# Products with stationary weights: one run of four loads per job instead of two runs of two

## What is computed

```
first_block:  h = x + (mixers(rms_norm(x) @ w_in, mem @ w_mem_kv) * gate) @ w_out
              u = relu(rms_norm(h) @ w_up)            # w_up   2048 x 8192
              h = h + (u * u) @ w_down                # w_down 8192 x 2048
second_block: m = hgrn2(rmsnorm(h) @ hgrn_w_in) @ hgrn_w_out
              x = h + rmsnorm(m)
              gate, value = conv3(rmsnorm(x) @ ffn_w_in)   # 2048 x 11264, centred, over tokens
              x = x + rmsnorm((silu(gate) * value) @ ffn_w_out)
```

## Time and profile before

| | |
|---|---|
| median of 3 runs | 2496.82 us (2496.26 to 2497.27) |
| the profiled execution | 2497.42 us |
| its span, first to last instruction | 2495.6 us |
| PE busy with matmuls | 2476.8 us, 99% of the span |
| PE loading weights | 2116.1 us, 85% |
| DVE busy | 1752.0 us, 70% |
| ACT busy | 1258.2 us, 50% |
| mean granted clock of PE | 0.997 |
| DMA | 466 MB, 187 GB/s |

### The profile page before, as it was taken

How to read it: one execution, slowest core, us unless ns; L and a number is a source line. 1 busy time by engine, 2 the same in 40 slices (tenths; PEclk the granted TensorE clock), 3 DMA queues, 4 the chain that set the end, 5 groups by cost and what they waited for, 6 DMA issues and landing times.

```text
span 2495.6 us, 38061 instructions
## 1 busy us (share of the span) xinstructions
PE 2476.8 (99%) x15416; PEld 2116.1 (85%) x15416; DVE 1752.0 (70%) x1978; ACT 1258.2 (50%) x1506; POOL 29.5 (1%) x26
## 2 busy tenths in 40 slices
PE   9999999999999999999999999999999999999998
PEld 7888888888888888888888888887888888888886
DVE  6656765668668577675777777775777666777777
ACT  7654344545444444445454545454654444444553
POOL 0000000000000000000000000000000000000000
PEclk9999999999999999999999999999999999999999
DMA  9454545546646546565545454555465555556553
GB/s 382 155 189 152 170 157 190 177 162 226 196 169 226 193 171 217 178 211 169 187 154 185 154 185 154 185 185 194 145 216 189 187 193 191 184 190 201 185 188 127
DMA packets 128240, 465.98 MB, mean 187 GB/s; under 512 B 14369, under 2 KB 14625, under 8 KB 127169
## 3 DMA queue, kind: packets, MB, share of 16 engines
q1 hardware_dynamic: 127920, 463.53, 55.1%
q10 hardware_dynamic: 144, 0.02, 0.0%
HBM read 461.39 MB, written 2.10 MB: 186 GB/s over the span
## 4 chain that ended last, share of the span: by engine, by line
PE 96%; issue 3%; DVE 1%; DMA 0%; ACT 0%; SPq 0%; DVEq 0%; POOL 0%; POOLq 0%
PE job L971 31%; PE job L983 16%; PE job L939 11%; PE job L940 11%; PE job L941 11%; PE job L958 2%; PE job L959 2%; PE job L960 2%; PE att L958 2%; PE att L960 2%; PE att L959 2%; PE att L1178 1%; PE att L999 0%; PE att L1011 0%; PE att L1120 0%
## 5 line engine op out<-in xcount | busy, mean ns | idle before, releaser
L1275 ACT ACTIVATE w_high<-raw 128x1024 fp32r<-128x1024 f32 (+1 forms) x883 | 919.8, 1050 | 728.4 <-PE job L941 288.5
L1594 DVE TENSOR_TENSOR w_low<-raw,w_high 128x1024 fp32r<-128x1024 f32 (+1 forms) x883 | 1045.4, 1213 | 303.9 <-ACT w_high L1275 225.9
L971 PE MATMUL job<-actA,w_high 128*128 128x512 f32 x3328 | 799.3, 392 | 0.0
L971 PEld LDWEIGHTS job<-actA,w_high 128*128 128x128 f32 x3328 | 612.8, 189 | 119.5
L983 PEld LDWEIGHTS job<-actA,w_low 128*128 128x128 f32 x3328 | 426.7, 191 | 16.2
L983 PE MATMUL job<-actA,w_low 128*128 128x256 f32 x3328 | 431.7, 283 | 0.0
L1797 DVE TENSOR_TENSOR slots<-job,slots 128x512 f32<-128x512 f32 x102 | 70.5, 691 | 344.0 <-ACT slots L1467 343.3
L939 PE MATMUL job<-w_high,actB 128*128 128x512 f32 x736 | 287.9, 391 | 2.2 <-DVE w_low L1594 1.6
L940 PE MATMUL job<-w_low,actB 128*128 128x512 f32 x736 | 286.5, 389 | 0.0
L941 PE MATMUL job<-w_high,actB 128*128 128x512 f32 x736 | 286.4, 389 | 0.0
L939 PE MATMUL job<-w_high,actA 128*128 128x512 f32 x576 | 230.9, 401 | 0.0
(11 more groups left out here) (257 smaller groups left out, 1906.1 us busy)
## 6 DMA issues: line engine op xcount, KB each, us to landing
raw<-in_weights SPq DMA_DIRECT2D x855, 512.0 KB, 4.2
M<-in_mem_t SPq DMA_DIRECT2D x8, 256.0 KB, 7.9
slots<-in_mem SPq DMA_DIRECT2D x2, 1024.0 KB, 12.2
M<-in_x_t SPq DMA_DIRECT2D x4, 512.0 KB, 13.6
H<-in_x SPq DMA_DIRECT2D x2, 1024.0 KB, 9.0
out<-H SPq DMA_DIRECT2D x8, 256.0 KB, 3.2
slots<-in_w_small SPq DMA_DIRECT2D x1, 1024.0 KB, 10.3
slots<-in_post_mix_g SPq DMA_DIRECT2D x1, 1024.0 KB, 4.8
```

The source lines that it names most:

```text
L971: mm = nc.tensor.matmul(J[job.buf][:, x, :], w_high[:, w % AHEAD, cols], act_both[job.act][:, c, :, :].rearrange("p a t -> p (a t)"), star ...
L1275: nc.scalar.activation(w_high[:, s % AHEAD, cols], raw[:, s % RAW_SLOTS, cols], ACT.Copy)\
L1594: nc.vector.tensor_tensor(w_low[:, s % AHEAD, cols], raw[:, s % RAW_SLOTS, cols], w_high[:, s % AHEAD, cols].bitcast(F32), ALU.subtract).t ...
```

## The change

In a `features` job all four wide products (32 matmuls) now come first, then all four narrow ones (32 matmuls): `together` is 4. Eight jobs keep runs of two: the first half of each result that waits for new activations (`needs`): four in the MLP's first block, two in hgrn's first group, two in the FFN's first block. The low parts move with it: where the window s-5 and the window s belong to `features` jobs with runs of four, the low part of s stands at s-2 (it was at s-4); where s belongs to another kind, the three low parts behind the first narrow products stand together at the job's third window. `splits` keeps the low parts in the order of their loads. `QUAD_ORDER` begins with two ordinary pairs (2 and 3) ahead of the first seven. The fourth `u_square` and `u_split` of an MLP block come one and three windows earlier. ACT's `y_split` no longer waits for all products up to its window but for the last down job that read the activations it overwrites.

```diff
-QUAD_ORDER = (("eight", 2), ("seven", 0), ("eight", 3), ("eight", 4), ("seven", 1), ("eight", 5), ("eight", 6), ("eight", 7))
+QUAD_ORDER = (("eight", 2), ("eight", 3), ("seven", 0), ("eight", 4), ("seven", 1), ("eight", 5), ("eight", 6), ("eight", 7))
...
+        self.together = self.windows if kind == "features" else 1
...
         j = p.job("features", act, weight, col + half * T, needs=needs)
+        if needs and half == 0:
+            j.together = 2
...
-            behind = 3 if j == 3 else 0
+            behind = 2 if j == 3 else 0
             p.put(job.end + behind, "u_square", j)
-            p.put(job.end + 1 + 2 * behind, "u_split", j)
+            p.put(job.end + 1 + behind + behind // 2, "u_split", j)
...
-def splits(late_ones):
-
-    at = {}
+def splits(late):
+
+    at, step = {}, -AHEAD
     for w in range(-AHEAD, PLAN.windows):
         for s in PLAN.splits.get(w, (w + AHEAD,)):
             if s < PLAN.windows:
-                late = int(s >= AHEAD and WINDOW[s - AHEAD][0].kind == "features" and late_ones(s))
-                at.setdefault(w + late, []).append(s)
-    return {w: sorted(splits) for w, splits in at.items()}
+                step = max(step, w, s - AHEAD + (late(s) if s >= AHEAD else 0))
+                at.setdefault(step, []).append(s)
+    return at
...
-    return splits(lambda s: True)
+    def late(s):
+        job, k = WINDOW[s - AHEAD]
+        if job.together < 4:
+            return job.together - 1
+        if WINDOW[s][0].kind == "features":
+            return 3
+        return max(2 - k, 0)
+    return splits(late)
...
                     wide(w).then_inc(wide_done, 1)
-                    if k % 2:
-                        narrow(w - 1).then_inc(window_done, 1)
-                        narrow(w).then_inc(window_done, 1)
+                    if (k + 1) % job.together == 0:
+                        for again in range(w + 1 - job.together, w + 1):
+                            narrow(again).then_inc(window_done, 1)
...
                     wait(act, n, "y_made", 0)
-                    act.wait_ge(window_done, w)
+                    act.wait_ge(window_done, DOWN_END.get(b - 2, 0) + 1)
```

More of the change, by code:

```diff
@@ L135, in __init__ @@
         self.halves = ()
+        self.down_end = {}
     def job(self, kind, act, weight, col, rows=range(KC), needs=None, offset=0):
@@ L467, in down @@
             banks[c] = j.buf
+        p.down_end[blocks[-1]] = j.end
     up("gate", 0)
@@ L497 @@
 plan_ffn(PLAN)
+DOWN_END = PLAN.down_end
 WINDOW = [(j, k) for j in PLAN.jobs for k in range(j.windows)]
@@ L537, in splits @@
             if s < PLAN.windows:
-                late = int(s >= AHEAD and WINDOW[s - AHEAD][0].kind == "features" and late_ones(s))
-                at.setdefault(w + late, []).append(s)
-    return {w: sorted(splits) for w, splits in at.items()}
+                step = max(step, w, s - AHEAD + (late(s) if s >= AHEAD else 0))
+                at.setdefault(step, []).append(s)
+    return at
 def low_splits():
-    return splits(lambda s: True)
+    def late(s):
[6 more added lines that the diff above has]
+    return splits(late)
 def high_splits():
-    return splits(lambda s: part_of(s) not in (None, 0))
+    return splits(lambda s: int(WINDOW[s - AHEAD][0].kind == "features" and part_of(s) not in (None, 0)))
 def walk(counts, window, split, stage, splits=None):
```

## The result

The changed kernel takes 2502.7 us (median of 12 runs, 2501.73 to 2505.14), the kernel before 2496.96 (12 runs, 2496.26 to 2500.2). The ratio is 1.0023, 95% interval 1.0015 to 1.0030: slower by 5.7 us, a little more than the 0.2% that a measurement tells from no change. Forecast were +4.9 us and 2501.7 us. The profiled execution took 2502.34, with a span of 2500.6.

What follows compares the result with a forecast made beforehand. PE bounds the kernel, busy 2476.8 of 2495.6 us, so only distances between matmuls and late arrivals count. The terms -1.9 + 3.5 + 2.5 + 0.75 = +4.9 us on the median 2496.82 gave 2501.7 us; range 2497.5 to 2506.0.

Steps and rivals of the forecast that it cites:

- Term 1: 96 features jobs with one run, not two: 0.02 us saved per change there and back, -1.9 us (0 to -2.9).
- Term 2: PE reaches `hgrn_across` before level 6's pick is done: about 1.2 us, three times, +3.5 us (3.3 to 4.0).
- Term 3: Low part behind `o_turn` and `f_make`, groups two to four, comes late: 0.85 us three times, +2.5 us (2.2 to 3.0).
- Term 4: First FFN value, low part behind `conv_side` and `y_mul`: fourth narrow product waits, +0.75 us once (0.65 to 0.9).
- At nothing: Places charged nothing, among them the gates (0.6 us early, ten times), `QUAD_ORDER`, earlier `u_square` and `u_split`, and `y_split`.
- the first seven's cover: Low part of the first seven's second load: 0.3 us of cover, gone with later low parts; the pair ahead returns 5.4.
- The second seven: Has less time behind the first seven: about 0.8 us of cover counted; had that gone, four blocks would pay.
- The clock: PE's gaps of about 1 us were charged nothing for the clock, whose mean is 0.997.
- No stalls, or one kind of them: Rivals: no stalls, only the first term left, 2494.9, chance 0.12; one kind only, 2499.2 or 2498.2, chance 0.08.
- Gates that stall: Rival, FFN gates: low part behind `conv_side` 1 us later, 0.4 us in ten blocks, 2505.7; chance 0.14.
- The order worth nothing: Rival: PE has the same distances in either order of wide and narrow, +6.8 us, 2503.6; chance 0.04.
- A gain beyond 0.2%: Rival: would need 0.07 us for each of the 96 changes with no stall at all; chance 0.03.

Runs made afterwards that it cites:

- experiment 1: Changed kernel with the first features job behind a group's tokens (groups two to four, three jobs) kept in pairs: 2498.4 us, ratio 1.0005.
- experiment 7: Changed kernel, all runs of four kept, with `hgrn_across` to `o_turn`, `f_make`, `conv_side` and `y_mul` moved to later windows: 2495.85 us, ratio 0.9992.
- Experiment 8: Kernel 3 with `conv_side` of the first value back where the change has it, only `y_mul` later: 2496.06 us, one execution.
- experiment 6: Kernel 3 with the old order of the quads, one ordinary pair ahead of the first seven: 2495.84 us, ratio 0.9993.
- 2: Changed kernel with `f_make` (direction 0, groups two to four) and the first value's `conv_side` one window later, `y_mul` two: 2498.78 us, ratio 1.0007.
- experiment 5: Runs of one: every features job takes wide and narrow products load by load, `together` 1 in the planner: 2501.05 us, ratio 1.0014.
- 3: Changed kernel with the diffs of experiments 1 and 2 together: 2495.15 us, ratio 0.9992.
- 4: Changed kernel with all features jobs in pairs, the rest of the change kept: 2497.12 us, ratio 1.0001.
- 12: Changed kernel with the old schedule of the low parts (10) and the three jobs behind tokens in pairs (experiment 1): 2495.04 us, ratio 0.9992.
- 9: Kernel 3 with the old order of the quads and the old places of `u_square` and `u_split`: 2495.48 us, ratio 0.9994.
- 10: Changed kernel with the low parts as before, at window s-4 and not s-2, under runs of four: 2499.14 us, ratio 1.0009.
- 11: Kernel 3 with the weaker wait of `y_split` undone: 2495.43 us, ratio 0.9994.

## Why the prediction was right

The mechanism was right in each of its four terms, and the size within about 0.1 us per place. Which side of 0.2% the result would fall on was left open (0.50 within, 0.47 slower by more); the forecast lay just within, and the result, +0.23%, just beyond.

**Term 1, fewer changes of width: right.** Forecast 0.02 us for each change there and back; the record shows 0.020, and runs of one give the same slope over twice the changes. So a fixed price per change is shown: the three kernels run the same 6656 matmuls of the jobs at 11.113, 11.133 and 11.173 us per job. The starts in the record to the nanosecond show where it lies, alike in runs of 8, 16 and 32: behind a narrow matmul the first five wide ones start 233, 236, 228, 232 and 231 ns apart and all later ones 227, which is 0.025 to 0.027 us more; the first narrow ones behind a wide one are 113 and 119 ns apart and all later ones 120, which gives back 0.007 to 0.008. The 0.03 and the 0.01 that I set against each other were thus right readings, but from rows rounded to 0.01, so the 0.02 could as well have been half or twice that, and it is in part luck that it came out.

The Trainium skill's formula for the gap (TensorE: Matmul & The Clock Gate, "Back-to-back issue gap"), N / 2.4 + 2.5 ns, has no term for the order, and the record shows one. The page gives that formula for an isolated matmul, which my prediction left out. For a stream with weight loads, as here, it gives about 131 ns at 512 columns. The 227 ns measured here, at a granted clock of 1.00, fit neither that nor the formula's 216.

**Term 2, `hgrn_across`: right in place and cause, 0.1 us short in size.** 1.31 us a place, 3.9 in all, for 1.2 and 3.5; inside the 3.3 to 4.0. The step was "the matmul can start at 1283.70, and would have at 1282.48 + 0.03", which takes a stall for the time until PE starts again. But the stage itself takes longer behind a stop: its 16 matmuls take 1284.64 - 1282.86 = 1.78 us to the next wide product, and 1285.11 - 1283.41 = 1.70 in experiment 1 (1290.02 - 1288.32 = 1.70 in experiment 7), where PE did not stop. The wait itself was 1.31 - 0.08 = 1.23.

**Term 3, behind `f_make`: right, with the same omission.** The fourth load was wanted at 1313.28 + 3 x 0.955 = 1316.15 and began at 1316.94: 0.79 of wait, where I had 0.85. The eight narrow matmuls behind the stop take 1318.00 - 1316.94 = 1.06 us in place of 0.955, another 0.10. Together 0.88 to 0.89, as the job's length says. The timeline of the changed kernel over the first matmul behind the stop shows where the 0.10 lies (PEld is PE's loading of weights):

```profile
1316.94 0.30 PEld L997 LDWEIGHTS job<-actA,w_low 128*128 128x128 f32 x2 [0.83 <-DVE w_low L1608]
1316.94 0.39 PE L997 MATMUL job<-actA,w_low 128*128 128x256 f32 x1 [0.63 <-DVE w_low L1608]
```

In the stream a matmul's weights are loaded while the matmul before it runs. Behind the stop the load had to wait for the low part too: it starts in the same 2 ns as its matmul, which is recorded with 0.39 us in place of the mean 0.283, and the next matmul starts 0.222 us behind it in place of 0.120; from there on the spacing is 0.117 to 0.120. It is the same at all four narrow stops (0.222 or 0.223), and alike at the three `hgrn_across` (0.184 or 0.185 in place of 0.108). So it is one long spacing, the first, and not a slow start over several matmuls. That the weight load is its cause fits all seven places and was not tried apart. The reading that DVE's time is unchanged there, since it hangs on ACT ahead of `o_turn`, held: the changed kernel has 1.90 us of wait in the same place as the earlier trace rows.

**Term 4: right.** 1812.05 + 2.87 = 1814.92 against 1815.62 is 0.70 of wait, and 1816.67 - 1815.62 = 1.05 holds another 0.10: 0.79 by the job's length, for 0.75. Experiment 8 shows which of the two stages does it.

**At nothing: right in the sum, wrong in a cover.** The gates did keep their 0.6 us (all ten jobs at 11.113). "This would be gone with low parts later", of the first seven's cover, was wrong: experiment 6 shows 2.1 us of cover there with the old order, since the sums moved too, and the join as what gets late, by 0.1 us. The second seven, for which I counted 0.8 us of cover, cost nothing: the `quads` of each MLP block take 84.35 us before and after (88.39 the last). The clock, charged at nothing, stayed at 1.00 through the stops. The order was read for the load whose wait I knew, and not for the stages that were pushed behind it.

**The rivals.** No stalls, or one kind of them: experiments 1 and 2 show both kinds. Gates that stall: none did. The order worth nothing: out by experiment 5. A gain beyond 0.2% was priced wrong, without consequence: 5.0 us over 96 changes is 0.05 us each, not 0.07.

**The sum.** The terms measured make -1.9 + 3.9 + 2.65 + 0.8 = 5.45 us; the forecast was 4.85, rounded to 4.9, and the medians show 5.7. The waits themselves, 3 x 1.23 + 3 x 0.79 + 0.70 = 6.76, are in sum what was forecast (6.75), the first a little more and the others a little less. The 0.6 between forecast and terms is what I had left out, the long first spacing behind seven stops: 3 x 0.08 + 4 x 0.10 = 0.64. The last 0.3 no row gives; it is within what executions differ by.

## What to carry to other kernels

When the bounding engine's instructions are reordered, list for every wait of that engine how long ago its releaser ended: a saving of 0.02 us in 96 places was outweighed by seven places where what PE needs was ready 0.7 to 1.2 us after PE's new arrival. Where another engine's deliveries are also put later, look at which stage now stands ahead of the delivery that is wanted last in the run; and try the reordering without the later deliveries first, since here they were not needed at all. A stop costs the wait and, here, 0.08 to 0.10 us more in the first spacing behind it.

## What the runs showed that was not expected

The long first spacing behind a stop, told above, is one such thing: 0.08 to 0.10 us, at a granted clock that did not fall.

The first job of the FFN differs by up to 1.1 us between executions, whatever the kernel. PE stands idle there for 3.8 us (the wait for `H`), and its clock is then low for a while. The stretches of the profile of before, with the granted clock in the last but two columns (us, busy us by engine, clock, DMA share, GB/s):

```profile
1751.00:1753.00 2.00, 2.00 (x9) 1.81 (x8) 2.00 (x7) 1.97 (x5) 0.00 (x0) 0.50 0.00 0
1753.00:1755.00 2.00, 2.00 (x7) 1.48 (x7) 2.00 (x7) 1.15 (x4) 0.00 (x0) 0.63 0.00 0
```

and of the changed kernel, whose transposes start at 1754.10 where those of before start at 1748.49:

```profile
1756.00:1758.00 2.00, 2.00 (x10) 1.89 (x9) 2.00 (x6) 1.98 (x6) 0.00 (x0) 0.52 0.00 0
1758.00:1760.00 2.00, 2.00 (x13) 1.65 (x12) 2.00 (x6) 1.00 (x4) 0.00 (x0) 1.00 0.00 0
```

0.50 is the lower of the clock's two levels, 1.2 GHz. In the profile of before it lasts until some 6 us behind the first transposes, in the changed kernel's until some 4. The eight wide matmuls behind the first transposes take 3.18 us to the next transposes in the one and 2.27 in the other. The -0.70 of the table comes from there, and it follows the execution and not the change: kernels 3, 4, 6 and 12 have it as before within 0.1 us, kernels 1, 2, 8, 9, 10 and 11 as the changed one, kernel 7 is between (-0.3), and runs of one had 1.2 less than before. Kernels 3, 8 and 11 differ from one another only behind this place, and 3 has it as before, the other two as the changed one. The first job of the program differs in the same way, by -1.1 to +2.1 us. So one profile of this kernel tells a total to about 1 us only, while the length of a job in mid-program repeats to 0.001 or 0.002 us: a change of 0.02 us in a job was plain in a single execution, where eleven timed runs did not settle 1.8 us in the total.
